# Two transformer blocks on one Trainium2 core: sums of squares moved and folded, a shorter final root, x's first pair on another queue

## What is computed

```python
# first block
x = x + 0.5 * swiglu(rms_norm(x, ffn1_norm), ...)          # gu0, down0
u = rms_norm(x, mix_norm) @ w_in                           # w_in: keys, values, queries, fourier features
q, k = rms_norm(q heads, q_norm), rms_norm(k heads, k_norm)   # 10 heads of 64
x = x + concat([fourier_mixer(...), gqa_attention(...)]) @ w_out
x = rms_norm(x + 0.5 * swiglu(rms_norm(x, ffn2_norm), ...), final_norm)   # gu1, down1
# second block, two layers
x = x + short_conv_mixer(rms_norm(x, norm_mix[0]))         # conv_in, conv_out
x = x + mem_cross_attention(...); x = x + swiglu_2(...)    # mem0, gu2, down2
x = x + moba_attention(rms_norm(x, norm_mix[1]), ...)      # moba
x = x + mem_cross_attention(...); x = x + swiglu_2(...)    # mem1, gu3, down3
return rms_norm(x, norm_final)

def rms_norm(x, g):
    return x * rsqrt(mean(x * x, axis=-1) + 1e-6) * g
```

## Time and profile before

| | us |
|---|---|
| median of 3 runs (lowest, highest) | 1262.18 (1260.85, 1262.86) |
| profiled execution | 1260.8 |
| its span | 1259.0 |
| TensorE busy | 1243.9 |
| VectorE busy | 925.3 |
| ScalarE busy | 657.5 |
| GpSimd busy | 30.9 |

### The profile page before, as it was taken

One profiled execution on the slowest core, in us unless ns is written; L12 is line 12 of the kernel. 1 busy time (PEld: TensorE's weight loads), 2 busy tenths in 40 slices (PEclk: granted clock), 3 DMA queues, 4 the chain that ended last, 5 costly groups with the idle time before them and its releaser, 6 DMA issues.

```text
span 1259.0 us, 18129 instructions
## 1 busy us (share of the span) xinstructions
PE 1243.9 (99%) x7458; PEld 1104.9 (88%) x7458; DVE 925.3 (73%) x1295; ACT 657.5 (52%) x867; POOL 30.9 (2%) x23
## 2 busy tenths in 40 slices
PE   8999999999999999999999999999999999999997
PEld 7888889878888888888888888889998888888886
DVE  7887856587877855988658777659977657877743
ACT  6655534364655543546546555545555445555432
POOL 0000000000000000440000000000000000000000
PEclk9999999999999999999999999999999999999998
DMA  8465754134555663555336555753435534555550
GB/s 312 174 227 186 230 190 164 68 106 163 200 179 189 200 235 128 173 197 173 136 137 228 201 179 190 226 176 135 168 135 182 186 134 139 200 197 192 192 185 34
DMA packets 51426, 221.74 MB, mean 176 GB/s; under 512 B 4464, under 2 KB 5776, under 8 KB 30864
## 3 DMA queue, kind: packets, MB, share of 16 engines
q1 hardware_dynamic: 51200, 220.52, 50.9%
q10 hardware_dynamic: 144, 0.07, 0.0%
HBM read 219.52 MB, written 1.05 MB: 175 GB/s over the span
## 4 chain that ended last, share of the span: by engine, by line
PE 91%; DVE 6%; ACT 1%; DMA 1%; issue 1%; SPq 0%; DVEq 0%; ACTq 0%
PE bank L405 48%; PE bank L435 21%; PE bank L409 7%; PE bank L426 4%; PE bank L474 2%; DVE wt L1153 2%; PE bank L685 2%; PE bank L713 2%; PE bank L451 1%; PE bank L477 1%; DVE xn L1162 1%; DVE x L1167 1%; PE bank L510 1%; DVE x L1168 1%; PE bank L456 1%; DMA x<-x_t 1%
## 5 line engine op out<-in xcount | busy, mean ns | idle before, releaser
L1153 DVE TENSOR_TENSOR wt<-raw,wt 128x2048 fp32r<-128x2048 f32 x202 | 464.1, 2299 | 69.0 <-ACT wt L831 68.6
L831 ACT ACTIVATE wt<-raw 128x2048 fp32r<-128x2048 f32 x202 | 385.9, 1911 | 125.4 <-PE bank L409 83.5
L405 PE MATMUL bank<-xn,wt 128*128 128x512 f32 x1712 | 417.3, 394 | 4.7 <-DVE xn L1162 4.1
L405 PEld LDWEIGHTS bank<-xn,wt 128*128 128x128 f32 x1712 | 314.1, 189 | 67.6 <-DVE xn L1162 6.7
L405 PE MATMUL bank<-h,wt 128*128 128x512 f32 (+1 forms) x1024 | 250.4, 393 | 0.0
L435 PEld LDWEIGHTS bank<-xn,wt 128*128 128x128 f32 x1856 | 239.3, 192 | 9.3
L435 PE MATMUL bank<-xn,wt 128*128 128x256 f32 x1856 | 242.9, 283 | 0.0
L405 PEld LDWEIGHTS bank<-h,wt 128*128 128x128 f32 (+1 forms) x1024 | 184.3, 188 | 35.7 <-issue 1.1
L1251 DVE TENSOR_TENSOR scratch<-bank,rest 128x512 f32<-128x512 f32 x98 | 67.6, 690 | 85.9 <-ACT rest L843 85.6
L906 ACT ACTIVATE h<-scratch 128x256 fp32r<-128x256 f32 x88 | 36.8, 418 | 158.8 <-DVE scratch L1291 158.8
L843 ACT ACTIVATE rest<-bank 128x512 f32<-128x512 f32 x114 | 67.6, 593 | 68.2 <-PE bank L435 67.9
(11 more groups left out here) (186 smaller groups left out, 961.6 us busy)
## 6 DMA issues: line engine op xcount, KB each, us to landing
raw<-weights SPq DMA_DIRECT2D x158, 1024.0 KB, 4.9
raw<-weights SPq DMA_DIRECT2D x88, 512.0 KB, 5.2
raw<-weights SPq DMA_DIRECT2D x8, 256.0 KB, 4.5
k_t<-mem_t SPq DMA_DIRECT2D x2, 1024.0 KB, 8.0
x<-x_t SPq DMA_DIRECT2D x4, 256.0 KB, 5.6
raw<-weights SPq DMA_DIRECT2D x8, 128.0 KB, 4.3
out_t<-work SPq DMA_DIRECT2D x4, 256.0 KB, 2.3
v_s<-fourier SPq DMA_DIRECT2D x2, 256.0 KB, 5.3
```

What stands on the lines that cost most here:

```text
L405: return pe.matmul(out, hi, a.rearrange("p a s -> p (a s)"), start=first, stop=False, skip_group_check=True)
L831: act.activation(wt[t % RING][:, 0], raw[t % RING][:], ACT.Copy).then_inc(weight_hi, 1)
L1153: dve.tensor_tensor(wt[t % RING][:, 1], raw[t % RING][:], wt[t % RING][:, 0].bitcast(F32), ALU.subtract).then_inc(weight_lo, 1)
```

## The change

Four places.

- Start: x's first pair is issued by ScalarE behind the vectors; both ScalarE and VectorE wait for the vectors only after their first piece of weights.
- Heads: each of the ten matmuls is a job of its own, ahead of blocks 5 and 6 of w_in's tile 2, and 2, 3, 4, 5 and 7 of tile 3 (four at the last).
- Convolution: mix0's squares are folded like the others, and a second block, `weighted` (the sum of the squares times final_norm squared), is made by VectorE; `both_sums` runs 4 one-column matmuls ahead of block 5 of conv_in's second tile.
- End: VectorE folds the first four blocks' squares into one; the low columns of the last bank are added to x before the last quarter, which `final_run` then accumulates in the high columns alone; the root is one of ScalarE's Sqrt and one Newton step on VectorE; seven matmuls of ones (KEEP = 7) stand between the last sums and the spread; the scaling of x by the gain is done in three parts (blocks 0 to 3, 4, and 5 to 7).

```diff
 SUM = {n: i for i, n in enumerate(SUMS)}
-FOLDED = [n for n in SUMS if n not in ("mix0", "final")]
+FOLDED = [n for n in SUMS if n != "final"]
...
         conv_s = [scratch[:, 0:2, :], scratch[:, 2:4, :]]
+        weighted = scratch[:, 0, :]
...
                 sp.dma_start(rows_of(raw[0][:], 2 * b, 2 * b + 2), rows_of(weights[0], 2 * b, 2 * b + 2)).then_inc(start_landed[b], 16)
-                sp.dma_start(x[:, pair(b), :], x_t[:, pair(b), :]).then_inc(x_landed[b], 16)
+                if b:
+                    sp.dma_start(x[:, pair(b), :], x_t[:, pair(b), :]).then_inc(x_landed[b], 16)
...
                     pe.wait_ge(spread_taken, SUM[name])
-                cols = 2 if name == "mix0" else 1
                 at = acc[0] if name == "final" else stat
-                blocks = [0] if name in FOLD else list(range(KB))
+                blocks = [0] if name in FOLD else [0, 4, 5, 6, 7] if name == "final" else list(range(KB))
...
                     pe.wait_ge(folded, FOLD[name] + 1)
+                if name == "final":
+                    pe.wait_ge(halved, 1)
                 for k in blocks[slice(*ks) if ks else slice(None)]:
-                    if name not in FOLD and k % 2 == 0:
+                    if name not in FOLD and k % 2 == 0 and (k or name != "final"):
...
                     for n in range(NT):
-                        mm = pe.matmul(at[:, 0, cols * n:cols * (n + 1)], work[:, k, n * P:(n + 1) * P],
-                                       weigh[:, k, 0:cols], start=k == 0 and n == 0, stop=k == blocks[-1], skip_group_check=True)
+                        mm = pe.matmul(at[:, 0, n:n + 1], work[:, k, n * P:(n + 1) * P],
+                                       weigh[:, k, 0:1], start=k == 0 and n == 0, stop=k == blocks[-1], skip_group_check=True)
...
                     mm.then_inc(summed, 1)
+            def both_sums():
+                pe.wait_ge(spread_taken, SUM["mix0"])
+                pe.wait_ge(folded, FOLD["mix0"] + 1)
+                for i, src in enumerate((work[:, 0, :], weighted)):
+                    for n in range(NT):
+                        mm = pe.matmul(stat[:, 0, 2 * n + i:2 * n + i + 1], src[:, n * P:(n + 1) * P], weigh[:, 0, 0:1],
+                                       start=i == n == 0, stop=i == 1, skip_group_check=True)
+                mm.then_inc(summed, 1)
...
                             mm.then_inc(acc_done, 1)
+                    return mm
+                def final_run(i):
+                    w, out = wt[(t0 + i) % RING], bank[:, 2 * PAIR[name, 3] + 1, 0:S]
+                    blocks = [(4 * n + 3, k) for n, k in enumerate(range(FF - 4, FF))]
+                    pe.wait_ge(lows_taken, 1)
+                    for at, k in blocks:
+                        for part in range(2):
+                            pe.matmul(out, w[:, 0, at, :], h[:, k, part, :], start=False, stop=False, skip_group_check=True)
+                    for at, k in blocks:
+                        mm = pe.matmul(out, w[:, 1, at, :], h[:, k, 0, :], start=False, stop=k == FF - 1, skip_group_check=True)
...
                         for m in range(4):
-                            mm = run(i, rows, 1, (m,), m == 0, rows[-1][1])
+                            if n_ffn == 3 and m == 3:
+                                mm = final_run(i)
+                            else:
+                                mm = run(i, rows, 1, (m,), m == 0, rows[-1][1])
...
-            def head_sums():
-                pe.wait_ge(qk_squared, 3)
-                for t in range(NT):
-                    for b in range(GQ_HEADS // 2):
-                        at = GQ_HEADS * t + 2 * b
-                        mm = pe.matmul(stat[:, 0, at:at + 2], qk_sq[b][:, t * P:(t + 1) * P], c("head_ones"),
-                                       start=True, stop=True)
-                mm.then_inc(qk_sum, 1)
+            def head_sum(b, t):
+                at = GQ_HEADS * t + 2 * b
+                pe.wait_ge(qk_squared, (b + 1) // 2 + 1)
+                mm = pe.matmul(stat[:, 0, at:at + 2], qk_sq[b][:, t * P:(t + 1) * P], c("head_ones"), start=True, stop=True)
+                if (b, t) == (GQ_HEADS // 2 - 1, NT - 1):
+                    mm.then_inc(qk_sum, 1)
+            def final_group():
+                for b, t in ((3, 0), (3, 1), (4, 0), (4, 1)):
+                    head_sum(b, t)
+            sums_beside = {2: {5: lambda: head_sum(0, 0), 6: lambda: head_sum(0, 1)},
+                           3: {2: lambda: head_sum(1, 0), 3: lambda: head_sum(1, 1), 4: lambda: head_sum(2, 0),
+                               5: lambda: head_sum(2, 1), 7: final_group}}
...
                 square_tile(FIRST["w_in"] + j, banks_for("w_in", j), xn, ready=operand("mix") if j == 0 else None, narrow=True,
-                            beside={**norm("mix"), 3: {5: head_sums}, 4: {4: head_factors}}.get(j, {}))
+                            beside={**norm("mix").get(j, {}), **sums_beside.get(j, {}), **({4: head_factors} if j == 4 else {})})
...
                 square_tile(FIRST["conv_in"] + j, banks_for("conv_in", j), xn, ready=operand("mix0") if j == 0 else None,
-                            beside={2: {1: lambda: spread_factor("mix0")}, 3: {1: lambda: spread_diagonal(DIAG["mix0 first"], 0)}}.get(j, {}))
-                if j == 0:
-                    sums("mix0")
+                            beside={1: {5: both_sums}, 2: {1: lambda: spread_factor("mix0")}, 3: {1: lambda: spread_diagonal(DIAG["mix0 first"], 0)}}.get(j, {}))
...
             gate_up(3, "ffn1")
-            down(3, "ffn1", {FF // 2 - 1: lambda: sums("final", (0, 4))})
-            sums("final", (4, KB))
+            down(3, "ffn1", {FF // 2 - 1: lambda: sums("final", (0, 1))})
+            sums("final", (1, 5))
+            for i in range(KEEP):
+                pe.matmul(stat[:, 1, 0:P], ones[:], ones[:], start=True, stop=True)
...
             act.dma_start(vec[:], vectors).then_inc(vec_landed, 16)
+            act.dma_start(x[:, pair(0), :], x_t[:, pair(0), :]).then_inc(x_landed[0], 16)
...
+            def gained(k0, k1):
+                for k in range(k0, k1):
+                    e = act.activation(q_t[:, k, :], x[:, k, :], ACT.Copy, scale=v("norm_final", k))
+                return e
...
                 after(t0 + FF // 2 - 2)
+                if not gain:
+                    gained(0, 4)
...
-            act.wait_ge(vec_landed, 16)
...
                 start(b, 0, 2 * b, 2 * b + 2, b == KP - 1)
+                if b == 0:
+                    act.wait_ge(vec_landed, 16)
...
             gate_up(3)
+            act.activation(table_s[:], ones[:, 0:NT], ACT.Sqrt)
             down(3, None, "final")
-            for k in range(KB):
-                e = act.activation(q_t[:, k, :], x[:, k, :], ACT.Copy, scale=v("norm_final", k))
-            e.then_inc(out_gained, 1)
+            gained(4, 5)
+            act.wait_ge(mean_whole, 1)
+            act.activation(root[:, 1, 0:NT], root[:, 0, 0:NT], ACT.Sqrt).then_inc(root_taken, 1)
+            gained(5, KB).then_inc(out_gained, 1)
...
                 e = add(out[:, 0:1], x[:, KB - 2:KB - 1, :], scale)
+                home, final = x[:, KB - 1:KB, :], out[:, 1:2]
...
                     e.then_inc(told, 1)
+                    dve.wait_ge(tile_done, FIRST[write] + FF // 2)
+                    dve.scalar_tensor_tensor(home, final[:, :, 0:S], scale, home, ALU.mult, ALU.add).then_inc(added, 1)
+                    return
                 dve.wait_ge(tile_done, FIRST[write] + FF // 2)
-                add(out[:, 1:2], x[:, KB - 1:KB, :], scale).then_inc(added, 1)
+                add(final, home, scale).then_inc(added, 1)
...
                     dve.tensor_tensor(work[:, 0, :], work[:, 0, :], work[:, 1, :], ALU.add).then_inc(folded, 1)
+            def weigh_pair(b):
+                dve.wait_ge(squared, KP * SUM["mix0"] + b + 1)
+                for k in (2 * b, 2 * b + 1):
+                    g = weigh[:, k, 1:2]
+                    if k == 0:
+                        link(dve.tensor_scalar(weighted, work[:, 0, :], g, None, ALU.mult))
+                    else:
+                        link(dve.scalar_tensor_tensor(weighted, work[:, k, :], g, weighted, ALU.mult, ALU.add))
...
                         rest_pair(name, i - 7, x, gain, xn)
+                if told == "mix0":
+                    weigh_pair(0)
+                    weigh_pair(1)
...
                     fold(told, 1)
+                if not gain:
+                    dve.wait_ge(squared, KP * SUM[name] + 2)
+                    link(dve.tensor_tensor(work[:, 0:2, :], work[:, 0:2, :], work[:, 2:4, :], ALU.add))
+                    dve.tensor_tensor(work[:, 0, :], work[:, 0, :], work[:, 1, :], ALU.add).then_inc(halved, 1)
+                    home, low = x[:, KB - 1, :], bank[:, 2 * PAIR[write, 3] + 1, S:2 * S]
+                    dve.wait_ge(tile_done, t0 + FF // 2 - 1)
```

(30 more changed lines are left out.)

2 lines of the change are left out of this document (added).

## The result

The changed kernel takes **1252.21 us** (median of five runs, 1251.46 to 1252.80) beside 1262.18 (1258.48 to 1262.86) of the kernel before, measured with it: ratio 0.9934, 95% interval 0.9923 to 0.9944, so 7.1 to 9.7 us less. (The two medians are 9.97 apart, outside that interval; the last experiment shows that the median of before stood high here.) The prediction was 1254.9 with a range of 1252.6 to 1257.5. The profiled execution took 1252.1 with a span of 1250.3, against 1260.8 and 1259.0: 8.7 less, where 7.35 had been worked out.

The account below looks back on a forecast made before the run. The prediction took TensorE, busy 99% of the span, as the bound, provided VectorE stays ahead. Gains of 0.4 + 0.9 + 2.95 + 3.1 = 7.35 us from 1262.2 gave 1254.9 us, range 1252.6 to 1257.5.

Parts of the forecast that it names:

- The start: Kernel start: x's first pair issued on ScalarE's queue, 0.4 us gained; bounds 0.6 gained or 0.3 lost.
- The heads: w_in's tiles 2 and 3: dealing out the sums ends a wait and a clock loss, net 0.9 us gained.
- The new wait: Tile 2 of w_in: TensorE waits 1.07 us for the keys' squares before the first pair of sums.
- rival D: Heads: the dealt-out sums still lower the clock, costing 1.35 us again, 1256.2 us in all; chance 8%.
- The convolution: Convolution's sums: folding the squares puts TensorE 4.2 us ahead, of which 2.95 us is kept.
- The give-back: Convolution: 1.25 us of TensorE's 4.2 us lead turns into a wait for weights on VectorE.
- the tightest meeting: Convolution's sixth weight tile: VectorE's split of the low half comes with 0.55 us of room before TensorE needs it.
- Rival A: Convolution: VectorE's order hides slack, so all 4.2 us stay, 1253.6 us in all; chance 15%.
- The end: After the last product: earlier sums 1.56, shorter root 0.9 and full-clock spread 0.65, together 3.1 us gained.
- Rival B: End: the ones run at 1.2 GHz and delay the spread, gaining 1.15 us there, 1256.9 in all; chance 12%.
- Rival C: End: ScalarE reloads its table at the root, 1.28 us on the path, 1256.2 in all; chance 8%.
- Rival E: Convolution's second tile: weighings hold back VectorE's split, making the kernel slower than before; chance 2%.

Follow-up runs that it names:

- the last experiment: The kernel before, unchanged, profiled once more: 1261.21 us; its 32 timed runs beside the experiments have a median of 1260.8 us.
- the early splits: Changed kernel with VectorE's splits of conv_in's fourth and sixth weight tiles moved ahead of its work on the tile before: 1252.31 us.
- the kernel with columns: Changed kernel with the convolution's norm summed column by column as before, without its weighings and folds on VectorE: 1256.73 us, ratio 0.9971.

## Why the prediction came out as it did

**The start, 0.4 worked out, 1.17 measured: the step that failed**, and with it more than half of the 1.37 by which the sum fell short of the profiles. I read the 0.88 share at 255 GB/s in the earlier trace rows as DMA engines nearly full, so that the bytes could not come sooner, and bounded the gain by one issue, 0.6. The experiments show that the engines were not full: with x's first pair on a second queue they move 307 to 344 GB/s in the stretch of 4 to 7 us (nine profiles), where one queue has 243 to 256 (four). The sign was in the trace of before, which moves 396 from 10 to 13 us. The upper bound was therefore no bound. The detail was wrong as well: the first wide product did not come 0.3 sooner, since the first piece of weights came 0.58 later.
The Trainium skill's page "DMA: Bandwidth & Descriptors", section "Issuing engines are not separate DMA queues", says that only the time to initiate a transfer is saved. The traces here differ: 1.17 and, over all profiles, 1.36 gained where one issue takes 0.6, with the throughput of that stretch up from 250 to 326 GB/s on average.

**The heads, 0.9 worked out, 1.10 measured.** The new wait was 1.00 (1.07 worked out) and the clock stayed full. The mechanism held, and rival D, a lowered clock in spite of the dealing out, did not come. One correction: a fall of the clock behind such a block is not certain, so dealing the sums out removes a chance of losing 1 to 3.5 us and costs 0.4 where the clock would have held.

**The convolution, 2.95 worked out, 3.34 measured.** Ahead of the third tile TensorE gained 4.17 (from 484.60 to 501.30 before, from 482.33 to 494.86 after) against 4.2, and VectorE 2.5 against 2.4 (502.52 to 497.79, less the 2.27 from earlier parts). The weighings and folds took 3.87 (485.40 to 489.27), as the 3.9 of the prediction, though the items that it lists add up to 3.6 or 3.7 only. The give-back was the mis-sized term: 1.25 worked out, all at the sixth tile; measured 0.83 net, as waits of 0.47 at the fourth and 0.64 at the sixth. I had looked for the tightest meeting at the sixth tile only. Rival A, no give-back, was wrong: VectorE is busy for 24.2 of 26 us, and the early splits only moved the waits. The ledger charges all of it as the fold's, which the kernel with columns confirms in sign and place, and in size only within the luck of the clock (4.96 where the clock fell for longer).

**The end, 3.1 worked out, 3.11 measured.** Term by term: VectorE's start on the sums 1249.81 to 1242.55, less the 5.61 gained before, is 1.65 (1.56 worked out); the steps of the root 2.16 to 1.21, 0.95 (0.9); the spread 1.80 to 1.29, 0.51 (0.65). Rival B, the ones at 1.2 GHz, was wrong: 14 records in 1.64 us. Rival C, a table load at the root, was wrong: the profile shows 0.20 us of root directly behind VectorE's step. Rival E had 1.3 us of room at the second tile, and no wait came.

**The median.** The forecast missed by 2.7: 1.37 lies in the terms and 1.3 in how the gain was carried over. The median of before then stood 1.4 above its profiled execution, that of the changed kernel stands 0.1 above its own, so the two medians are 9.97 apart and the profiles 8.7. I took the 1.4 as a constant; it was chance in which executions of before were drawn, as its other medians (1260.1 to 1261.1) show.

So all four terms had the right sign, three were within 0.4, and all errors went one way. The range failed at its low end: it had allowed only 0.6 for the start, and half a microsecond for the median. (As its parts are named, that end adds up to 1252.95 rather than 1252.6.)
